# Linear attention: the squares of the outputs summed on ScalarE, the gated outputs in a buffer of their own

## The chip, the cores and the metric

The kernel runs on one core of a Trainium2 chip. The metric is the device time of one execution in microseconds (us), lower is better. Engines are named TensorE (PE), VectorE (DVE), ScalarE (ACT), GpSimd (POOL) and SyncE (SP, which here only starts transfers).

## What is computed

One layer of a hybrid decoder, for a prompt of 1024 tokens with 16 meta tokens in front and for 8 decode sequences of 4 new tokens each. A projection feeds two groups of heads: four heads of gated linear attention and eight heads of latent attention. Their outputs go through an output projection, a layer norm, a gated feed-forward with a short convolution, and another layer norm. The change touches the linear attention alone, which in the reference is:

```python
def gla_chunked(q, k, v, log_a, s0, chunk):
    ...
    def step(s, inp):
        qi, ki, vi, gi = inp
        b = jnp.cumsum(gi, axis=2)
        ...
        o_inter = jnp.einsum('bhcd,bhde->bhce', qi * jnp.exp(b), s)
        att = jnp.einsum('bhid,bhjd->bhij', qi * jnp.exp(b - b_mid), ki * jnp.exp(b_mid - b))
        att = jnp.where(causal, att, 0.0)
        o_intra = jnp.einsum('bhij,bhje->bhie', att, vi)
        s_new = s * jnp.exp(b_last)[:, :, 0, :, None] + jnp.einsum(
            'bhcd,bhce->bhde', ki * jnp.exp(b_last - b), vi)
        return s_new, o_inter + o_intra
...
def mixer_output(o_gla, g_g, o_lat, gla_norm_g, w_uv, w_o):
    gate = jax.nn.silu(g_g.reshape(B, T, GLA_HEADS, GLA_DV))
    og = (rms_norm(o_gla, gla_norm_g) * gate).reshape(B, T, GLA_HEADS * GLA_DV)
```

The root-mean-square norm of each head's output (128 values) needs the sum of its squares; the norm's factor and the gate are both multiplied onto the output.

## The kernel before

The program is written out by hand for each engine: one function per stage and engine (`pe_c`, `act_c`, `dve_c`, `pool_c` are the linear attention), called one after another. An engine runs its instructions in the order in which they are written and stops at `wait_ge(semaphore, count)` until the count is reached. So the order within an engine is fixed, and all order between engines is by semaphores. `dve_settle` and `act_settle` make an engine wait for its own last instruction before the next one.

The linear attention has nine tiles of tokens. Tile 0 has 48 rows (32 decode tokens and the 16 meta tokens), tiles 1 to 8 have 128 prompt tokens each, which are two reference chunks of 64. I call a tile a chunk below. For chunk i:

- TensorE: `scores(i)` (L707) and transposes of the decayed keys (L714); `outputs(i)` from the masked scores and the values (L738) and from the states (L751; L744 for chunk 0); `updates(i)`, the two state products (L724; L782 for chunk 0); `turn(i)`, transposes of the finished outputs (L762). From i = 2 on its order is scores(i), outputs(i-1), updates(i), turn(i-2).
- ScalarE: `kdt_copy(i)` (L811) brings the turned keys out of PSUM; `o_copy(i)` (L820) the outputs, in two instructions, into `osb[i % 2]`; `og_copy(i)` (L827) the turned outputs into `catT` with the norm's gain. Order: kdt_copy(i), o_copy(i-1), og_copy(i-2).
- VectorE: `mask(i)` (L867) copies the scores under the causal mask into `att`; `squares(i)` squares the outputs into `sq` (L891), sums each head's 128 squares into `orow` (L894) and multiplies the gate onto the outputs in place (L895); `states(i)` (L879) decays and updates the state twice; `scale(i)` (L901) multiplies the norm's factor on. Order: mask(i), squares(i-1), states(i), scale(i-1).
- GpSimd: two small instructions per chunk (L934, L935) turn the sums into the factor, from `osum_ready` to `orstd_ready`. After chunk 0 it also starts the two stores of the decode states.

`outputs(i)` waits for the masked scores of chunk i, for `o_copy(i-1)` (`osb_ready`), and for the first of the two state updates in `states(i)` (`state_ready`). The waits in it:

```python
                pe.wait_ge(att_masked, 2 * (i + 1))
                if i >= 1:
                    pe.wait_ge(osb_ready, 2 * i)
                    pe.wait_ge(state_ready, 2 + 2 * (i - 1) + 1)
```

A sum of squares on ScalarE exists elsewhere in the kernel: at L569, `ACT.Square` with `accum_out`, on rows of 384 and 256 elements, closed by a one-element copy at L571 that raises the semaphore. `accum_out` becomes an instruction of its own, ACTIVATION_READ_ACCUMULATOR. The latent attention's softmax (L1302) also uses `accum_out`. The stage after this one starts with VectorE's L1127 and TensorE's L1040, which both wait for the last `og_copy` (`og_out`).

Of the kernel before, what the change touches and what calls it, by code (L numbers as in the profile page):

```python
# [8 lines left out]
ACT = mybir.ActivationFunctionType  # L9
AX = mybir.AxisListType  # L10
# [4 lines left out]
P = 128  # L15
# [36 lines left out]
def rows(i):  # L52
    return ROWS0 if i == 0 else P
# [49 lines left out]
def build(nc, ins, outs):  # L103
    with ExitStack() as ctx:
# [541 lines left out]
        qbz = at("qbz", [P, 2, DEC_B, ROWS0], E0 + 14912)  # L646
        sq = at("sq", [P, GH, GV], E0 + 17984)
        orow = at("orow", [P, 2, 8], E0 + 20032)
# [48 lines left out]
        def pe_c(pe):  # L697
# [58 lines left out]
            def turn(i):  # L756
                r = rows(i)
                pe.wait_ge(og_ready, i + 1)
                if i >= 1:
                    pe.wait_ge(og_out, i)  # L760
                for h in range(GH):
                    last = nc.tensor.transpose(ps[:, 7, P * h:P * h + r], osb[i % 2][0:r, h // 2, h % 2, :],  # L762
                                               ident[0:r, 0:r])
                last.then_inc(og_turned, 1)
# [36 lines left out]
        def act_c(act):  # L801
# [12 lines left out]
            def o_copy(i):  # L814
                r = rows(i)
                act.wait_ge(o_done, i + 1)
                if i >= 2:
                    act.wait_ge(og_turned, i - 1)
                for h in range(2):
                    nc.scalar.activation(osb[i % 2][0:r, :, h, :],  # L820
                                         ps[0:r, 4 + h, 0:256].rearrange("p (m e) -> p m e", m=2),
                                         ACT.Copy).then_inc(osb_ready, 1)

            def og_copy(i):
# [10 lines left out]
            last.then_inc(vz_act, 1)  # L835
            o_copy(0)
            kdt_copy(1)
            for i in range(1, NT + 2):
                if 2 <= i < NT:
                    kdt_copy(i)  # L840
                if 1 <= i - 1 < NT:
                    o_copy(i - 1)
                if 0 <= i - 2 < NT:
                    og_copy(i - 2)

        def dve_c(dve):
# [37 lines left out]

            def squares(i):
                r = rows(i)
                dve.wait_ge(osb_ready, 2 * (i + 1))
                x = osb[i % 2][0:r, :, :, :].rearrange("p m h e -> p (m h) e")
                if i >= 1:
                    dve.wait_ge(osum_ready, i)  # L890
                dve_settle(nc.vector.tensor_tensor(sq[0:r, :, :], x, x, mult))  # L891
                if i >= 2:
                    dve.wait_ge(og_ready, i - 1)
                nc.vector.tensor_reduce(orow[0:r, i % 2, 0:4], sq[0:r, :, :], AX.X, add).then_inc(osum_ready, 1)  # L894
                dve_settle(nc.vector.tensor_tensor(x, x, gate_t[0:r, i, :].rearrange("p (h e) -> p h e", h=GH), mult))  # L895

            def scale(i):
                r = rows(i)
                x = osb[i % 2][0:r, :, :, :].rearrange("p m h e -> p (m h) e")
                dve.wait_ge(orstd_ready, i + 1)  # L900
                nc.vector.tensor_tensor(x, x, orow[0:r, i % 2, 4:8].unsqueeze(2).broadcast_to((r, GH, GV)),  # L901
                                        mult).then_inc(og_ready, 1)
# [6 lines left out]
            mask(1)  # L909
            squares(0)  # L910
            dve.wait_ge(o_done, 1)
# [10 lines left out]
            for i in range(2, NT + 1):  # L922
                if i < NT:
                    mask(i)
                squares(i - 1)
                if i < NT:
                    states(i)
                scale(i - 1)
# [1432 lines left out]
```

## Time and profile before

| | |
|---|---|
| median of 3 runs | 1787.85 us (1786.32 to 1788.46) |
| profiled execution, its own time | 1788.77 us |
| its span | 1787.0 us |
| mean granted TensorE clock | 0.951 of full speed |
| TensorE busy (matmul) | 1631.3 us, 91% |
| VectorE busy | 735.3 us, 41% |
| ScalarE busy | 586.9 us, 33% |
| GpSimd busy | 211.6 us, 12% |

The span is the time between the first and the last instruction in the trace; the execution's own time has some 1.8 us around it. Busy shares are means over stages that differ: the linear attention runs from about 266 to 340 us of the span, 4% of it. Times in the trace are us from the span's start. In a timeline row the number in square brackets is how long the engine had been idle before, and behind `<-` what released it; "x4" says that four like instructions are merged in the row.

### The profile page before, as it was taken

How to read it: one execution, taken by the hardware profiler on the slowest of the kernel's cores; microseconds unless marked ns; L12 is line 12 of the kernel's file. 1: busy time of each engine (PE TensorE's matmuls, PEld its weight loads, DVE VectorE, ACT ScalarE, POOL GpSimd, SP SyncE). 2: the span in 40 equal slices, each digit the busy share in tenths (PEclk: the TensorE clock that was granted, in tenths of full speed). 3: DMA queues.
4: the chain of work that ended last, by engine and by line, in shares of the span. 5: the costliest groups of instructions: out<-in, count | busy, mean ns of one | idle time of the engine just before them, and what ended most of it. 6: DMA issues, size and time to landing. Idle time of an engine off the chain costs nothing.

```text
span 1787.0 us, 26293 instructions
## 1 busy us (share of the span) xinstructions
PE 1631.3 (91%) x10609; PEld 1377.2 (77%) x10609; DVE 735.3 (41%) x1297; ACT 586.9 (33%) x1090; POOL 211.6 (12%) x313
## 2 busy tenths in 40 slices
PE   4999997898999787888979999999999979989994
PEld 4989995565666454446869999999999978768783
DVE  7325007655555333335651222222222234364744
ACT  2246212333566544442112222222222223233330
POOL 2110002103400355211110000000000000010101
PEclk9999998798999988888989999999999989999997
DMA  7202112011100555441231111111111134354530
GB/s 239 103 31 63 48 29 71 4 47 47 32 1 1 195 174 193 142 142 73 93 107 37 39 43 47 47 47 35 47 47 47 35 118 141 118 175 125 180 119 27
DMA packets 91169, 147.73 MB, mean 83 GB/s; under 512 B 6346, under 2 KB 63048, under 8 KB 91048
## 3 DMA queue, kind: packets, MB, share of 16 engines
q1 hardware_dynamic: 75242, 92.84, 16.5%
q0 software_dynamic: 15408, 52.30, 8.7%
q10 hardware_dynamic: 432, 1.37, 0.2%
q8 instruction: 62, 1.02, 0.2%
q14 instruction: 25, 0.20, 0.0%
HBM read 130.76 MB, written 15.72 MB: 82 GB/s over the span
## 4 chain that ended last, share of the span: by engine, by line
PE 67%; DVE 4%; ACT 3%; issue 1%; DMA 1%; POOL 0%; SPq 0%; ACTq 0%; DVEq 0%; POOLq 0%
PE ps L208 16%; PE ps L210 16%; PE ps L209 16%; PE ps L1241 4%; PE ps L1575 4%; PE ps L1555 3%; PE ps L1278 2%; PE ps L1601 2%; PE ps L1255 2%; ACT pastr L1652 2%; DVE d_lo L2206 1%; DVE y L306 1%; DVE y L308 1%; DVE wo_lo L1825 0%; DVE y L2185 0%
## 5 line engine op out<-in xcount | busy, mean ns | idle before, releaser
L210 PE MATMUL ps<-h1T_hi,f_lo 128*128 128x358 f32 (+1 forms) x1056 | 344.5, 326 | 0.0
L209 PE MATMUL ps<-h1T_lo,f_hi 128*128 128x358 f32 (+1 forms) x1056 | 344.3, 326 | 0.0
L208 PE MATMUL ps<-h1T_hi,f_hi 128*128 128x358 f32 (+1 forms) x1056 | 343.4, 325 | 0.0
L208 PEld LDWEIGHTS ps<-h1T_hi,f_hi 128*128 128x128 f32 x1056 | 199.3, 189 | 0.0
L210 PEld LDWEIGHTS ps<-h1T_hi,f_lo 128*128 128x128 f32 x1056 | 199.3, 189 | 0.0
L209 PEld LDWEIGHTS ps<-h1T_lo,f_hi 128*128 128x128 f32 x1056 | 199.1, 189 | 0.0
L208 PE MATMUL ps<-d_hi,g_hi 128*128 128x512 f32 x396 | 159.0, 402 | 19.2 <-DVE d_lo L2206 16.4
L209 PE MATMUL ps<-d_lo,g_hi 128*128 128x512 f32 x396 | 158.0, 399 | 0.0
L210 PE MATMUL ps<-d_hi,g_lo 128*128 128x512 f32 x396 | 157.8, 398 | 0.0
L208 PE MATMUL ps<-w_hi,hT_hi 128*128 128x256 f32 (+2 forms) x504 | 140.9, 280 | 0.0
L210 PE MATMUL ps<-w_hi,hT_lo 128*128 128x256 f32 (+2 forms) x504 | 140.3, 278 | 0.0
L209 PE MATMUL ps<-w_lo,hT_hi 128*128 128x256 f32 (+2 forms) x504 | 140.3, 278 | 0.0
L2038 DVE TENSOR_TENSOR f_lo<-f_raw,f_hi 128x1024 fp32r<-128x1024 f32 x44 | 53.7, 1221 | 201.3 <-ACT f_hi L1991 201.3
L2051 DVE SCALAR_TENSOR_TENSOR conv<-ext,vcol,conv 128x1088 f32<-128x1088 f32 x44 | 59.5, 1352 | 151.7 <-ACT conv L2023 148.7
L1991 ACT ACTIVATE f_hi<-f_raw 128x1024 fp32r<-128x1024 f32 x44 | 46.2, 1052 | 211.7 <-PE ps L210 197.6
L208 PEld LDWEIGHTS ps<-d_hi,g_hi 128*128 128x128 f32 x396 | 75.3, 190 | 40.0 <-issue 14.5
L210 PEld LDWEIGHTS ps<-w_hi,hT_lo 128*128 128x128 f32 x504 | 96.4, 191 | 0.0
L208 PEld LDWEIGHTS ps<-w_hi,hT_hi 128*128 128x128 f32 x504 | 96.2, 191 | 0.1
L209 PEld LDWEIGHTS ps<-w_lo,hT_hi 128*128 128x128 f32 x504 | 95.9, 190 | 0.0
L2204 DVE TENSOR_TENSOR g_lo<-gT,g_hi 128x384 fp32r<-128x384 f32 (+1 forms) x88 | 38.2, 455 | 139.9 <-ACT d_hi L2168 139.9
L2167 ACT ACTIVATE g_hi<-gT 128x384 fp32r<-128x384 f32 (+1 forms) x88 | 36.6, 439 | 178.5 <-PE ps L210 172.1
L210 PEld LDWEIGHTS ps<-d_hi,g_lo 128*128 128x128 f32 x396 | 75.3, 190 | 18.4
(297 smaller groups left out, 2755.5 us busy)
## 6 DMA issues: line engine op xcount, KB each, us to landing
d_raw<-in_w_down SPq DMA_DIRECT2D x66, 512.0 KB, 3.6
f_raw<-in_w_ffn_in SPq DMA_DIRECT2D x88, 256.0 KB, 3.2
w_raw<-in_w_in SPq DMA_DIRECT2D x6, 1024.0 KB, 5.2
xs<-in_x_prompt SPq DMA_DIRECT2D x8, 512.0 KB, 4.2
h_res<-xs POOLq DMA_DIRECT2D x8, 512.0 KB, 4.0
wo_raw<-in_w_o SPq DMA_DIRECT2D x2, 2048.0 KB, 8.7
hr<-h_res SPq DMA_DIRECT2D x8, 512.0 KB, 3.7
h_res<-hr POOLq DMA_DIRECT2D x8, 512.0 KB, 3.0
```

Of the source, the lines that this page charges most:

```text
L208: nc.tensor.matmul(out, ah, bh, start=start, stop=False)
L209: nc.tensor.matmul(out, ah, bl, start=False, stop=False)
L210: return nc.tensor.matmul(out, al, bh, start=False, stop=stop)
L1241: last = nc.tensor.matmul(ps[:, bank + b, 0:w], qT[0:QD, h, c:c + P], kT[0:QD, h, NS + 512 * b:NS + 512 * b + w], start=True, stop=True)
L1255: last = nc.tensor.transpose(ps[:, 4 + g % 2, P * t:P * t + P], probs[k % 2][:, P * b:P * b + P], ident)
L1555: last = nc.tensor.transpose(ps[:, n % TURN_BANKS, P * j:P * j + P], src, ident)
L1575: last = nc.tensor.matmul(ps[32 * b:32 * b + 32, bank, 0:n], q, x, start=c == 0, stop=c == 2)
L1991: nc.scalar.activation(f_hi[h][:, :, :, :], f_raw[h][:, :, :, :], ACT.Copy).then_inc(f_high, 1)
L2038: nc.vector.tensor_tensor(f_lo[h][:, :, :, :], f_raw[h][:, :, :, :], f_hi[h][:, :, :, :].bitcast(F32), sub).then_inc(f_split, 1)
L2051: last = nc.vector.scalar_tensor_tensor(out=conv[:, :], in0=ext[:, j:j + LC], scalar=vcol[:, bass.ds(c + V_ROWS["conv_w"] + j * FC, 1)], i ...
L2167: nc.scalar.activation(g_hi[m % SPL][:, o:o + n], gT[:, k, c:c + n], ACT.Copy)
L2204: nc.vector.tensor_tensor(g_lo[m % SPL][:, o:o + n], gT[:, k, c:c + n], g_hi[m % SPL][:, o:o + n].bitcast(F32), sub)
```

## The change

Three things change, all in the linear attention.

- The squares and their sums go from VectorE to ScalarE. A function `squares` in `act_c`, right behind each `o_copy`, issues four `ACT.Square` of 128 columns (one per head) with `accum_out` into `orow`, each followed by a wait on itself, and a one-element copy that raises `osum_ready`. The result of the Squares themselves goes to a scratch tile, `sq_junk`.
- The gated outputs go to a pair of buffers of their own, `ogb`, in place of `osb` in place. `scale` and TensorE's transposes work on `ogb`.
- The waits follow: `o_copy(i)` waits for `og_ready` (chunk i-2 scaled) where it waited for `og_turned` (chunk i-2 turned); the new `squares(i)` for the same; VectorE's `gated(i)`, which replaces its `squares(i)`, waits for `og_turned` (chunk i-2 turned).

```diff
--- before.py
+++ after.py
@@ -644,7 +644,8 @@
         osb = [at(f"osb{i}", [P, 2, 2, GV], E0 + 8384 + 2048 * i) for i in range(2)]
         kdt = [at(f"kdt{i}", [P, 2, P], E0 + 12864 + 1024 * i) for i in range(2)]
         qbz = at("qbz", [P, 2, DEC_B, ROWS0], E0 + 14912)
-        sq = at("sq", [P, GH, GV], E0 + 17984)
+        ogb = [at(f"ogb{i}", [P, 2, 2, GV], o) for i, o in enumerate((E0 + 17984, E0 + 47168))]
+        sq_junk = at("sq_junk", [P, GV], E0 + 49216)
         orow = at("orow", [P, 2, 8], E0 + 20032)
         sst = [at(f"sst{i}", [P, 2, GV], E0 + 21440 + 1024 * i) for i in range(4)]
 
@@ -759,7 +760,7 @@
                 if i >= 1:
                     pe.wait_ge(og_out, i)
                 for h in range(GH):
-                    last = nc.tensor.transpose(ps[:, 7, P * h:P * h + r], osb[i % 2][0:r, h // 2, h % 2, :],
+                    last = nc.tensor.transpose(ps[:, 7, P * h:P * h + r], ogb[i % 2][0:r, h // 2, h % 2, :],
                                                ident[0:r, 0:r])
                 last.then_inc(og_turned, 1)
 
@@ -815,11 +816,20 @@
                 r = rows(i)
                 act.wait_ge(o_done, i + 1)
                 if i >= 2:
-                    act.wait_ge(og_turned, i - 1)
+                    act.wait_ge(og_ready, i - 1)
                 for h in range(2):
                     nc.scalar.activation(osb[i % 2][0:r, :, h, :],
                                          ps[0:r, 4 + h, 0:256].rearrange("p (m e) -> p m e", m=2),
                                          ACT.Copy).then_inc(osb_ready, 1)
+
+            def squares(i):
+                r = rows(i)
+                if i >= 2:
+                    act.wait_ge(og_ready, i - 1)
+                for h in range(GH):
+                    last = act_settle(nc.scalar.activation(sq_junk[0:r, :], osb[i % 2][0:r, h // 2, h % 2, :], ACT.Square,
+                                                           accum_out=orow[0:r, i % 2, h:h + 1]))
+                nc.scalar.activation(sq_junk[0:r, 0:1], osb[i % 2][0:r, 0, 0, 0:1], ACT.Copy).then_inc(osum_ready, 1)
 
             def og_copy(i):
                 r, c = rows(i), col0(i)
@@ -834,12 +844,16 @@
                                             ACT.Identity, scale=consts[0:ROWS0, C_SEG + s:C_SEG + s + 1])
             last.then_inc(vz_act, 1)
             o_copy(0)
+            act.wait_ge(osb_ready, 2)
+            squares(0)
             kdt_copy(1)
             for i in range(1, NT + 2):
                 if 2 <= i < NT:
                     kdt_copy(i)
                 if 1 <= i - 1 < NT:
                     o_copy(i - 1)
+                    act.wait_ge(osb_ready, 2 * i)
+                    squares(i - 1)
                 if 0 <= i - 2 < NT:
                     og_copy(i - 2)
 
@@ -882,21 +896,18 @@
                     last.then_inc(state_ready, 1)
                     dve.wait_ge(state_ready, 2 + n + 1)
 
-            def squares(i):
+            def gated(i):
                 r = rows(i)
                 dve.wait_ge(osb_ready, 2 * (i + 1))
-                x = osb[i % 2][0:r, :, :, :].rearrange("p m h e -> p (m h) e")
-                if i >= 1:
-                    dve.wait_ge(osum_ready, i)
-                dve_settle(nc.vector.tensor_tensor(sq[0:r, :, :], x, x, mult))
                 if i >= 2:
-                    dve.wait_ge(og_ready, i - 1)
-                nc.vector.tensor_reduce(orow[0:r, i % 2, 0:4], sq[0:r, :, :], AX.X, add).then_inc(osum_ready, 1)
-                dve_settle(nc.vector.tensor_tensor(x, x, gate_t[0:r, i, :].rearrange("p (h e) -> p h e", h=GH), mult))
+                    dve.wait_ge(og_turned, i - 1)
+                dve_settle(nc.vector.tensor_tensor(ogb[i % 2][0:r, :, :, :].rearrange("p m h e -> p (m h) e"),
+                                                   osb[i % 2][0:r, :, :, :].rearrange("p m h e -> p (m h) e"),
+                                                   gate_t[0:r, i, :].rearrange("p (h e) -> p h e", h=GH), mult))
 
             def scale(i):
                 r = rows(i)
-                x = osb[i % 2][0:r, :, :, :].rearrange("p m h e -> p (m h) e")
+                x = ogb[i % 2][0:r, :, :, :].rearrange("p m h e -> p (m h) e")
                 dve.wait_ge(orstd_ready, i + 1)
                 nc.vector.tensor_tensor(x, x, orow[0:r, i % 2, 4:8].unsqueeze(2).broadcast_to((r, GH, GV)),
                                         mult).then_inc(og_ready, 1)
@@ -907,7 +918,7 @@
                                                consts[0:ROWS0, C_SEG + s:C_SEG + s + 1], None, mult)
             last.then_inc(vz_ready, 1)
             mask(1)
-            squares(0)
+            gated(0)
             dve.wait_ge(o_done, 1)
             for m in range(2):
                 dve.wait_ge(u_done, m + 1)
@@ -922,7 +933,7 @@
             for i in range(2, NT + 1):
                 if i < NT:
                     mask(i)
-                squares(i - 1)
+                gated(i - 1)
                 if i < NT:
                     states(i)
                 scale(i - 1)
```

**VectorE, one prompt chunk in the steady part, before.** `sq` and `osb` are the squares and the outputs, `sst` the states, `att` the masked scores:

```order
L891 TENSOR_TENSOR sq<-osb_108 128x512 [waits osum_ready,osb_ready]
L894 TENSOR_REDUCE orow<-sq 128x4 [waits og_ready,dve_step]
L895 TENSOR_TENSOR osb_108<-osb_108,gate_t 128x512
L879 SCALAR_TENSOR_TENSOR sst_116<-sst_115,ebl,ps 128x128 [waits o_done,u_done,dve_step]
L879 SCALAR_TENSOR_TENSOR sst_116<-sst_115,ebl,ps 128x128
L879 SCALAR_TENSOR_TENSOR sst_117<-sst_116,ebl,ps 128x128 [waits o_done,u_done,state_ready]
L879 SCALAR_TENSOR_TENSOR sst_117<-sst_116,ebl,ps 128x128
L901 TENSOR_TENSOR osb_108<-osb_108,orow 128x512 [waits orstd_ready,state_ready]
L867 COPY_PREDICATED att_106<-gmask,ps 128x128 [waits o_done,att_done]
```

**VectorE, the same place now.** `ogb` is the new buffer of gated outputs:

```order
L904 TENSOR_TENSOR ogb_113<-osb_108,gate_t 128x512 [waits og_turned,osb_ready]
L893 SCALAR_TENSOR_TENSOR sst_118<-sst_117,ebl,ps 128x128 [waits o_done,u_done,dve_step]
L893 SCALAR_TENSOR_TENSOR sst_118<-sst_117,ebl,ps 128x128
L893 SCALAR_TENSOR_TENSOR sst_119<-sst_118,ebl,ps 128x128 [waits o_done,u_done,state_ready]
L893 SCALAR_TENSOR_TENSOR sst_119<-sst_118,ebl,ps 128x128
L912 TENSOR_TENSOR ogb_113<-ogb_113,orow 128x512 [waits orstd_ready,state_ready]
L881 COPY_PREDICATED att_106<-gmask,ps 128x128 [waits o_done,att_done]
```

Two instructions and the waits between them are gone in front of the state updates; the scale and the mask behind it stand where they stood, and the scale still waits for `orstd_ready`.

**ScalarE, the same kind of chunk, before:**

```order
L811 ACTIVATE kdt_110<-ps 128x256 [waits u_done,kd_turned]
L820 ACTIVATE osb_109<-ps 128x2x128 [waits og_turned,o_done]
L820 ACTIVATE osb_109<-ps 128x2x128
L827 ACTIVATE catT<-ps,vcol 128x4x128 [waits og_turned]
```

**ScalarE now:**

```order
L812 ACTIVATE kdt_110<-ps 128x256 [waits u_done,kd_turned]
L821 ACTIVATE osb_109<-ps 128x2x128 [waits og_ready,o_done]
L821 ACTIVATE osb_109<-ps 128x2x128
L830 ACTIVATE sq_junk,orow<-osb_109 128x128 [waits og_ready,osb_ready]
L830 ACTIVATE sq_junk,orow<-osb_109 128x128 [waits act_step] x3
L832 ACTIVATE sq_junk<-osb_109 128x1 [waits act_step]
L837 ACTIVATE catT<-ps,vcol 128x4x128 [waits og_turned]
```

Between the copy of the outputs and the copy of turned outputs there are five more instructions (and an accumulator read after each of the four Squares, which this view doesn't list).

## Rows read from the trace of the kernel before

**Rows 1.** The page, part 4: shares of the span by engine.
```profile
PE 67%; DVE 4%; ACT 3%; issue 1%; DMA 1%; POOL 0%; SPq 0%; ACTq 0%; DVEq 0%; POOLq 0%
```

**Rows 2.** Stretch, its us; busy PE, PEld, DVE, ACT, POOL; PEclk, DMA, GB/s.
```profile
291.50:334.20 42.70, 32.95 (x359) 24.25 (x352) 31.99 (x80) 11.45 (x28) 11.00 (x14) 0.86 0.09 29
```

**Rows 3.** Timeline of one prompt chunk: start us, duration us, engine, line, operation.
```profile
303.06 0.66 ACT L820 ACTIVATE osb<-ps 128x256 f32<-128x256 f32 x2 [2.55 <-PE ps L751]
...
303.75 0.69 DVE L891 TENSOR_TENSOR sq<-osb 128x512 f32<-128x512 f32 x1 [0.82 <-ACT osb L820]
...
304.65 0.44 PE L714 MATMUL ps<-consts,t_b 128*128 128x128 f32 x2
...
305.08 0.68 DVE L895 TENSOR_TENSOR osb<-osb,gate_t 128x512 f32<-128x512 f32 x1
...
305.80 1.25 DVE L879 SCALAR_TENSOR_TENSOR sst<-sst,ebl,ps 128x128 f32<-128x128 f32 x4
...
306.55 0.68 PE L738 MATMUL ps<-v_t,att 128*128 128x128 f32 x4 [1.46 <-DVE sst L879]
...
307.08 0.69 DVE L901 TENSOR_TENSOR osb<-osb,orow 128x512 f32<-128x512 f32 x1
...
307.69 0.89 DVE L867 COPY_PREDICATED att<-gmask,ps 128x128 f32<-128x128 int32 x4
...
308.70 0.66 ACT L820 ACTIVATE osb<-ps 128x256 f32<-128x256 f32 x2 [3.19 <-PE ps L751]
```

**Rows 4.** Timeline of ScalarE: the other six output copies of prompt chunks.
```profile
290.94 0.66 ACT L820 ACTIVATE osb<-ps 128x256 f32<-128x256 f32 x2 [2.92 <-PE ps L751]
...
297.42 0.66 ACT L820 ACTIVATE osb<-ps 128x256 f32<-128x256 f32 x2 [4.15 <-PE ps L751]
...
315.72 0.66 ACT L820 ACTIVATE osb<-ps 128x256 f32<-128x256 f32 x2 [4.58 <-PE ps L751]
...
321.36 0.66 ACT L820 ACTIVATE osb<-ps 128x256 f32<-128x256 f32 x2 [3.10 <-PE ps L751]
...
327.65 0.66 ACT L820 ACTIVATE osb<-ps 128x256 f32<-128x256 f32 x2 [3.84 <-PE ps L751]
...
333.52 0.66 ACT L820 ACTIVATE osb<-ps 128x256 f32<-128x256 f32 x2 [3.25 <-PE ps L751]
```

**Rows 5.** Timeline of ScalarE at 106 to 121 us: Squares with an accumulator.
```profile
108.05 0.53 ACT L569 ACTIVATE junk<-zt 128x384 f32<-128x384 f32 x1
...
108.69 0.42 ACT L569 ACTIVATE junk<-zt 128x256 f32<-128x256 f32 x1
...
109.24 0.52 ACT L569 ACTIVATE junk<-zt 128x384 f32<-128x384 f32 x1
...
118.76 0.20 ACT L571 ACTIVATE junk<-zt 128x1 f32<-128x1 f32 x1
```

**Rows 6.** Groups of ScalarE by line and shape: busy us, mean ns | idle.
```profile
L1302 ACT ACTIVATION_READ_ACCUMULATOR probs<-ps,mx 128x1 f32 x66 | 13.3, 201 | 0.0
...
L1302 ACT ACTIVATE probs<-ps,mx 128x128 f32<-128x128 f32 x8 | 2.9, 365 | 0.0
```

**Rows 7.** Timeline where the stage starts (chunk 0).
```profile
276.48 0.65 ACT L820 ACTIVATE osb<-ps 48x256 f32<-48x256 f32 x2 [5.33 <-PE ps L744]
...
277.37 4.09 PE L782 MATMUL ps<-vz,kdt 48*64 48x512 f32 x24
...
279.94 2.15 DVE L915 SCALAR_TENSOR_TENSOR s_in<-s_in,ebl,ps 128x128 f32<-128x128 f32 x8
```

**Rows 8.** Timeline where the stage ends.
```profile
334.94 0.69 DVE L894 TENSOR_REDUCE orow<-sq 128x4 f32<-128x512 f32 x1
...
335.71 0.56 POOL L934 TENSOR_SCALAR orow<-orow 128x4 f32<-128x4 f32 x1 [4.22 <-DVE orow L894]
...
337.46 0.69 DVE L901 TENSOR_TENSOR osb<-osb,orow 128x512 f32<-128x512 f32 x1 [1.25 <-POOL orow L935]
...
340.08 0.49 DVE L1127 TENSOR_SCALAR w_uqn<-w_uq_sb,vcol 128x512 f32<-128x512 f32 x1 [1.93 <-ACT catT L827]
```

## The prediction

> **What bounds the kernel now.** I read four views in this order. The chain that ended last comes first: 67% of the span is TensorE [rows 1]. The change touches only the linear attention stage, so I ask whether TensorE sets the pace there too. The busy time by stretch says no: over the eight prompt chunks TensorE has work in 33.0 of 42.7 us, VectorE in 32.0, ScalarE in 11.5 [rows 2]. No engine is full, so the chunk runs at the pace of a loop of waits. The timeline of one chunk shows the loop [rows 3]: ScalarE copies the outputs (303.06, 0.66 us); VectorE squares them (303.75), sums, gates (305.08), then updates the states (305.80); TensorE, which waited for the first state, starts the next outputs (306.55); the next copy starts at 308.70. Period: 5.64 us.
>
> The stretches of this loop, from the same rows: copy start to square 0.69; square to gate 1.33 (square and row sum); gate to state update 0.72; state update to TensorE 0.75; TensorE to the next copy 2.15. Gate start to next copy start is thus 3.62.
>
> Not every chunk has this pace. The eight copies start at 290.94, 297.42, 303.06, 308.70, 315.72, 321.36, 327.65 and 333.52 [rows 3, 4]: periods of 6.48, 5.64, 5.64, 7.02, 5.64, 6.29, 5.87. Less 0.69 + 1.33 = 2.02, the parts from gate start to next copy are 4.46, 3.62, 3.62, 5.00, 3.62, 4.27 and 3.85. The longer ones are TensorE's at a lower clock: 0.86 granted in this stretch [rows 2], so about a quarter of it ran at 1.2 GHz and the rest at 2.4.
>
> **The change, part by part.**
>
> *Removed from VectorE:* square and row sum, 1.33 us of the loop per chunk. If nothing took their place, the loop would be 5.64 - 1.33 = 4.31 us at the full clock; seven periods give 9.3 us.
>
> *Added to ScalarE:* four Square instructions of 128 elements, each followed by its accumulator read and a wait on itself, and a one-element copy that signals. The same construction runs earlier in the kernel with 384 and 256 elements [rows 5]: start to start 0.64 (108.05 to 108.69) and 0.55 (108.69 to 109.24), read and wait included. 128 elements fewer cost 0.10, so at 128 I take 0.445 each, 1.78 for four. The one-element copy takes 0.20. Upper bound: the shortest activation with an accumulator, 128 elements out of PSUM, takes 0.365, and its read 0.201 [rows 6]: 0.566. Lower bound: 0.33, one of the two 256-element halves of the output copy without accumulator. The three differ mostly in overlap; I take 0.445 because it is the same instruction, operand memory and wait.
>
> *Where that lies:* ScalarE has room: busy 11.45 us in the eight chunks, 1.4 each [rows 2], and 1.98 more makes 3.4 of 4.31; and the next output copy waits for TensorE. But the row sums now come later. From a copy's start: 0.66 copy, 0.03 hand-over (as 303.72 to 303.75), 1.78 squares, 0.20 signal, 0.08 to GpSimd: 2.75. GpSimd's two instructions and the hand-over take 1.75 (335.71 to 337.46) [rows 8], so VectorE can scale that chunk 4.50 us after the copy began. It is ready for it much sooner (the state updates end some 0.69 + 0.72 + 1.25 = 2.7 us after it), so **a new wait appears**: VectorE stands at the scale for up to 1.9 us, where before GpSimd's answer was in before it came there. Behind the scale in VectorE's order stand the mask of the chunk after next and then the next chunk's gate. Scale to mask is 0.61, the mask 0.89 (307.08, 307.69) [rows 3]. So the next chunk's gate can't start before 4.50 + 1.50 = 6.00 us after the previous chunk's copy began. With gate to copy 3.62 this is a loop over two chunks of 6.00 + 3.62 = 9.62, or 4.81 each. It is longer than 4.31 and sets the average pace.
>
> *The walk, with the measured TensorE parts.* Gate = the later of (own copy + 0.69) and (previous copy + 6.00); next copy = gate + its part. From a first copy at 290.50 (next paragraph) the copies come at 295.65, 300.12, 305.27, 311.12, 315.42, 321.39 and 325.93. Before, the last was at 333.52, so this is 7.59 earlier, 0.44 of it from the start of the stage.
>
> *Start of the stage.* Chunk 0 loses 1.33 us in front of VectorE's first big update at 279.94, but that also waits for TensorE's first six pairs of state products: 24 matmuls of 4.09 us from 277.37, so half are done at 279.4 [rows 7]. Gain: 0.44, not 1.33. ScalarE's copy of chunk 1's keys now stands behind four squares: 277.13 + 0.03 + 1.98 + 0.33 = 279.5. TensorE wants it at 279.4; lost 0.1, off VectorE's path. The first prompt chunk's copy starts at 290.94 - 0.44 = 290.50.
>
> *End of the stage.* After the last copy (333.52) the row sum ends at 334.94 + 0.69, and the scale starts at 337.46, 3.94 after the copy [rows 4, 8]. Now 4.50: lost 0.56. After that ScalarE's last copy and the next stage follow directly: VectorE's first instruction there (340.08) waited for that copy [rows 8], so the shift is handed on whole.
>
> *The buffer of its own and the swapped waits* cost nothing: the transpose reads the new buffer at the same place in each order, and the copy's new condition (the chunk two back is scaled) is met before the gate of the chunk in between. No transfer is added.
>
> **Sum:** -0.44 (start) - 7.15 (seven periods) + 0.56 (end) = -7.0 us. The profiled execution took 1788.77 in all (span 1787.0), giving 1781.8; it lay 0.9 above the median of the runs shown, 1787.85, from which I forecast **1780.8**.
>
> **A rule weighed against the rows.** In rows 5 the Squares take 0.53 and 0.42 us; the slope leaves about 0.32 for 128 elements without the accumulator read. The Trainium skill (VectorE: DVE Perf Modes, the section on the TRN2 errata) gives a ScalarE instruction from SBUF 224 cycles plus one per element, an estimate of 0.29 us here, and warns that many small tiles pay the fixed part each time. By 0.29 a Square, with its read wholly hidden, the walk would give 9.0 us gained and 1778.8 in place of 1780.8; by the rows the read isn't hidden, so the rows' sum stays.
>
> **The rivals.**
>
> 1. *The wait at the scale hardly binds, or TensorE speeds up.* Without the 6.00 bound the same walk gives 9.2 us (1778.7). With the bound but TensorE at 2.4 GHz all the way (3.62 each) it gives 9.3. Both together would give 12.3 (1775.6). For it: TensorE's idle gaps shrink. Against: 4.50 is built from measured pieces. Chance 0.15.
>
> 2. *TensorE becomes the bound, or a Square costs the upper price.* At the full clock TensorE finishes the last transposes of a chunk's scores at 305.09 (304.65 + 0.44), 2.03 after the copy's start, while the shortened loop wants its next outputs at 0.69 + 1.47 = 2.16: only 0.13 to spare, none at 1.2 GHz. With 0.566 per Square the gain is 4.9 us; with all seven parts at 5.00, 2.6. That is 1783.0 to 1785.3. Chance 0.12.
>
> 3. *Slower than before: VectorE is held at the scale longer than it saved.* Place: the scale in VectorE's order, behind ScalarE's squares and GpSimd. Each extra 0.1 us per Square lengthens the two-chunk loop by 0.4 and the end by 0.4; it also holds up ScalarE's copy of chunk 1's keys at the start. The walk turns from gain to loss at about 0.82 us per Square, and at 1.0 gives +3.8, 1791.6. It would take Squares delayed by VectorE's gate reading the same tile at that moment. Against: no activation with accumulator of this size takes over 0.57 with its read. The Trainium skill (ScalarE: Activation LUTs, the rules for kernel authors) says to keep multiplications off ScalarE; that points this way, and no row of this case bears it out at this size. Chance 0.03.
>
> 4. *The gain is given back.* The next stages start 7 us earlier, and TensorE's lower clock falls on other work, or a transfer isn't there yet. Time 1787 to 1788. Against: the first instructions of the next stage wait for ScalarE, not for a transfer [rows 8]. Chance 0.05.
>
> The forecast itself has 0.65.
>
> **How the numbers follow.** Differences under 0.2% (3.6 us) can't be told from none: the border is 1784.3. Faster: 0.65 + 0.15 + half of the second rival (0.06) = 0.86. Within: the other 0.06 + 0.05 = 0.11. Slower: 0.03. The range reaches down to 1777.0, past most of the first rival, and up to 1784.5, into the second, which leaves out somewhat under 2 in 10.
>
> **What would show it.** Per chunk: four Squares with reads in about 1.8 us; VectorE idle before the scale, ended by GpSimd, some 1 to 1.9 us in most chunks; gate starts alternating between 4.3 and 5.4 us apart; first copy to last 35.4 us in place of 42.6; the last copy to the last scale 4.5. The forecast is wrong if the average period is under 4.6 or over 5.6, or if the stage is 7 us shorter and the span isn't.

## The result, and the profile after

The changed kernel took 1776.22 us (median of 6 runs, 1771.75 to 1779.43) beside 1787.41 (6 runs, 1782.21 to 1788.46) for the kernel before: ratio 0.994, 95% interval 0.9921 to 0.9958. Two later groups of runs gave 0.9933 (0.9908 to 0.9957) and 0.9933 (0.9912 to 0.9955). It is faster, as forecast, but by 11 us and not by 7: the median lies 0.8 us under the range (1777.0 to 1784.5). The profiled execution took 1779.43.

The page as a whole hardly moved. Its part 1 and the first line of part 4:

```profile
PE 1628.7 (92%) x10609; PEld 1375.9 (77%) x10609; DVE 723.0 (41%) x1279; ACT 601.4 (34%) x1171; POOL 208.1 (12%) x313
...
PE 67%; DVE 4%; ACT 3%; issue 1%; DMA 1%; POOL 0%; SPq 0%; ACTq 0%; DVEq 0%; POOLq 0%
```

ScalarE has 14.5 us more work and 81 instructions more, VectorE 12.3 us less, and the chain is TensorE's for the same 67% [rows 1]. The stage says more. Its busy time over the eight prompt chunks (same columns as [rows 2]: length, PE, PEld, DVE, ACT, POOL, then PEclk, DMA share, GB/s):

```profile
292.60:324.40 31.80, 27.95 (x355) 20.17 (x350) 22.40 (x66) 22.77 (x91) 8.43 (x14) 1.00 0.12 39
```

The stretch is 31.8 us long where it was 42.7, and the granted clock is 1.00 where it was 0.86. TensorE has work in 28.0 of 31.8 us. One pair of periods in the timeline of the changed kernel, to be laid beside [rows 3]:

```profile
301.17 0.66 ACT L821 ACTIVATE osb<-ps 128x256 f32<-128x256 f32 x2 [1.36 <-PE ps L752]
...
301.86 0.69 DVE L904 TENSOR_TENSOR ogb<-osb,gate_t 128x512 f32<-128x512 f32 x1
...
301.86 0.31 ACT L830 ACTIVATE sq_junk<-osb 128x128 f32<-128x128 f32 x1
...
302.07 0.19 ACT L830 ACTIVATION_READ_ACCUMULATOR sq_junk<-osb 128x1 f32 x1
...
302.29 0.31 ACT L830 ACTIVATE sq_junk<-osb 128x128 f32<-128x128 f32 x1
...
303.34 0.68 PE L739 MATMUL ps<-v_t,att 128*128 128x128 f32 x4
...
303.59 0.20 ACT L832 ACTIVATE sq_junk<-osb 128x1 f32<-128x1 f32 x1
...
303.88 0.19 POOL L945 TENSOR_SCALAR orow<-orow 128x4 f32<-128x4 f32 x1 [3.54 <-ACT sq_junk L832]
...
304.15 1.01 POOL L946 TENSOR_TENSOR orow<-orow,mhalf 128x4 f32<-128x4 f32 x1
...
305.27 0.69 DVE L912 TENSOR_TENSOR ogb<-ogb,orow 128x512 f32<-128x512 f32 x1 [1.44 <-POOL orow L946]
...
305.49 0.66 ACT L821 ACTIVATE osb<-ps 128x256 f32<-128x256 f32 x2 [0.84 <-PE ps L752]
...
305.87 0.89 DVE L881 COPY_PREDICATED att<-gmask,ps 128x128 f32<-128x128 int32 x4
...
306.67 0.68 DVE L904 TENSOR_TENSOR ogb<-osb,gate_t 128x512 f32<-128x512 f32 x1
...
307.39 1.25 DVE L893 SCALAR_TENSOR_TENSOR sst<-sst,ebl,ps 128x128 f32<-128x128 f32 x4
...
308.14 0.68 PE L739 MATMUL ps<-v_t,att 128*128 128x128 f32 x4 [0.24 <-DVE sst L893]
...
308.20 0.19 POOL L945 TENSOR_SCALAR orow<-orow 128x4 f32<-128x4 f32 x1 [3.04 <-ACT sq_junk L832]
...
310.29 0.66 ACT L821 ACTIVATE osb<-ps 128x256 f32<-128x256 f32 x2 [1.32 <-PE ps L752]
```

Two periods of three engines stand here, row by row in order of time. The gate (L904) starts 0.69 us after the copy (L821), with no square and row sum in front of it. The Squares come every 0.43 us. VectorE then stands at the scale for 1.44 us until GpSimd is done (305.27), does the mask (305.87), and only then, at 306.67, the next gate, though its copy began at 305.49. The periods are 4.32 (301.17 to 305.49) and 4.80 (305.49 to 310.29). All seven: 4.32, 4.84, 4.32, 4.80, 4.32, 4.80, 4.32, in all 31.72 us; before 42.58 [rows 3, 4]. The mean period is 4.53 us, under the 4.6 that the prediction named as a sign of being wrong.

The end of the stage, in the same view:

```profile
323.73 0.66 ACT L821 ACTIVATE osb<-ps 128x256 f32<-128x256 f32 x2 [1.12 <-PE ps L752]
...
327.83 0.69 DVE L912 TENSOR_TENSOR ogb<-ogb,orow 128x512 f32<-128x512 f32 x1 [2.72 <-POOL orow L946]
...
330.45 0.49 DVE L1138 TENSOR_SCALAR w_uqn<-w_uq_sb,vcol 128x512 f32<-128x512 f32 x1 [1.93 <-ACT catT L837]
```

From the last copy to the last scale it takes 4.10 us (3.94 before), and the next stage starts 2.62 us later, as before (337.46 to 340.08) [rows 8].

### The profile page after: what moved, and what is told of

Same layout as the page of the kernel before. It is cut to its first block, busy times and chain, and to the rows that moved or that the text cites. A ratio compares the mean times of both kernels' runs of the same rounds, so it can differ in the third digit from the quotient of the medians.

```text
span 1777.6 us, 26355 instructions
## 1 busy us (share of the span) xinstructions
PE 1628.7 (92%) x10609; PEld 1375.9 (77%) x10609; DVE 723.0 (41%) x1279; ACT 601.4 (34%) x1171; POOL 208.1 (12%) x313
## 4 chain that ended last, share of the span: by engine, by line
PE 67%; DVE 4%; ACT 3%; issue 1%; DMA 1%; POOL 0%; SPq 0%; ACTq 0%; DVEq 0%; POOLq 0%
PE ps L208 16%; PE ps L210 16%; PE ps L209 16%; PE ps L1252 4%; PE ps L1586 4%; PE ps L1566 4%; PE ps L1289 2%; PE ps L1612 2%; PE ps L1266 2%; ACT pastr L1663 2%; DVE d_lo L2217 1%; DVE y L306 1%; DVE y L308 1%; DVE wo_lo L1836 0%; DVE y L2196 0%
## 5 line engine op out<-in xcount | busy, mean ns | idle before, releaser
L208 PEld LDWEIGHTS ps<-d_hi,g_hi 128*128 128x128 f32 x396 | 75.5, 191 | 39.8 <-issue 14.5
```

Of the source, the lines that this page charges most:

```text
L208: nc.tensor.matmul(out, ah, bh, start=start, stop=False)
```

## The experiments

Three groups of runs followed the result, each beside the kernel before on its own chip: before and changed again, slowed and mask first; then buffers alone, gate in place, Squares twice and square beside GpSimd; then changed a third time, mask first again, order alone and states first. "Copies" is the time from the start of the first to the start of the last output copy of the eight prompt chunks, seven periods, in the profiled execution of each; "clock" is TensorE's granted clock from the end of the first copy to the start of the last; "out" is the start of the next stage's first VectorE instruction.

| kernel | median us | ratio to before (95%) | copies us | clock | out us |
|---|---|---|---|---|---|
| before | 1787.41 | | 42.58 | 0.87 | 340.08 |
| before again | 1786.43 | 0.9991 (0.9971 to 1.0012) | 44.80 | 0.80 | 341.54 |
| changed | 1776.22 | 0.9940 (0.9921 to 0.9958) | 31.72 | 1.00 | 330.45 |
| changed again | 1774.55 | 0.9933 (0.9908 to 0.9957) | 31.73 | 1.00 | 327.56 |
| changed, third | 1773.46 | 0.9933 (0.9912 to 0.9955) | 31.73 | 1.00 | 328.73 |
| slowed | 1787.15 | 1.0008 (0.9986 to 1.0029) | 44.11 | 0.85 | 343.19 |
| buffers alone | 1885.21 | 0.9992 (0.9969 to 1.0015) | 40.51 | 0.96 | 336.31 |
| gate in place | 1893.26 | 1.0036 (1.0017 to 1.0055) | 49.28 | 0.82 | 346.83 |
| Squares twice | 1888.20 | 1.0007 (0.9984 to 1.0029) | 39.26 | 0.94 | 341.67 |
| square beside GpSimd | 1875.07 | 0.9942 (0.9922 to 0.9961) | 33.33 | 1.00 | 331.93 |
| mask first | 1773.28 | 0.9928 (0.9903 to 0.9952) | 30.24 | 1.00 | 327.74 |
| mask first again | 1774.83 | 0.9940 (0.9919 to 0.9960) | 30.25 | 1.00 | 329.13 |
| order alone | 1779.12 | 0.9971 (0.9956 to 0.9987) | 34.61 | 0.95 | 334.96 |
| states first | 1768.38 | 0.9906 (0.9884 to 0.9928) | 28.42 | 1.00 | 327.29 |

The kernel before had medians of 1786.91, 1885.84 and 1784.63 in the three groups. The chip of the second group ran every kernel 5 to 6% longer. Later stages held the stalls that were seen (with the buffers alone ScalarE's L1306 sat idle for 18.9 us at once), and their cause was not looked for. Of this group the ratios and the copies are used, not the times.

**1. Before and changed, once more.** No edit. The question is whether the low clock in the chunks belongs to the kernel before.

> The kernel before, unchanged, timed against itself and profiled once more. Question: were the long TensorE parts of its chunks (first to last output copy 42.58 us, 39.5 if all were at 2.4 GHz) its own, or the chance of one execution? Theory A (TensorE idles enough in each 5.6 us period that its clock drops again and again): the mean granted clock between the first and the last copy of the prompt chunks is again clearly under 1.00, and copy to copy 41 to 44 us. Theory B (chance of the moment): it may be 1.00, and 39.5 us. Time 1787 us, ratio 1.000 within 0.002.

> The changed kernel, unchanged, timed and profiled once more. Theory A: granted clock 1.00 between the first and last output copy again, seven periods alternating between 4.32 and 4.82 us, 31.7 us in all. Theory B: some low stretches, 32 to 35 us. GpSimd's first instruction 0.19 us again. Time 1776 us, ratio to before 0.994.

> The changed kernel a third time: ratio to before 0.9935 within 0.002; the granted clock in the chunks 1.00, periods alternating between 4.32 and 4.8 us, 31.7 us for the seven.

Busy time between the first and the last copy, before again:

```profile
290.84:334.98 44.14, 34.56 (x349) 25.41 (x348) 31.98 (x80) 10.69 (x26) 11.01 (x14) 0.80 0.08 28
```

The changed kernel again:

```profile
289.77:320.84 31.07, 27.31 (x348) 19.71 (x344) 21.93 (x66) 22.06 (x88) 8.45 (x14) 1.00 0.12 40
```

The clock is 0.80 in one and 1.00 in the other, as in the first pair, and 1.00 in the third profile of the changed kernel. The long periods of the kernel before fell elsewhere (7.17, 5.64, 6.49, 5.64, 5.64, 7.04, 7.18), but they are there again. Its shortest period is 5.64 both times. Theory A, that the low clock belongs to this loop and not to the chance of one execution, stands.

**2. Slowed.** The removed work is put back in front of the gate, into tiles that nobody reads:

```diff
             def gated(i):
...
+                x = osb[i % 2][0:r, :, :, :].rearrange("p m h e -> p (m h) e")
+                dve_settle(nc.vector.tensor_tensor(sqd[0:r, :, :], x, x, mult))
+                dve_settle(nc.vector.tensor_reduce(sumd[0:r, 0:GH], sqd[0:r, :, :], AX.X, add))
                 dve_settle(nc.vector.tensor_tensor(ogb[i % 2][0:r, :, :, :].rearrange("p m h e -> p (m h) e"),
```

> The changed kernel with VectorE's square and row sum put back in front of the gate, into tiles nobody reads (the computation is unchanged otherwise). The loop is 5.64 us again, TensorE idles as before. Theory A (the clock follows from TensorE's idle share): the granted clock between first and last copy falls under 1.00 again, 41 to 44 us, and the whole kernel is back at 1786 to 1788 us. Theory B (chance): clock 1.00, 39.5 us, about 1784 us.

```profile
293.01:336.46 43.45, 32.80 (x349) 23.95 (x350) 32.64 (x80) 22.17 (x88) 8.44 (x14) 0.85 0.09 28
```

Theory A came: clock 0.85, copies 44.11 us, and the whole kernel back at 1787.15. Only the shortest period is not 5.64 as expected but 5.76. The whole gain hangs on the length of this loop. Seven periods of 5.76 would be 40.3 us; nearly all of the other 3.8 lie in three periods of 6.77 to 7.25, in which the granted clock was 0.75 to 0.82.

**3. Mask first.** VectorE's next mask moves into the idle time before the scale:

```diff
+            mask(2)
             for i in range(2, NT + 1):
-                if i < NT:
-                    mask(i)
                 gated(i - 1)
                 if i < NT:
                     states(i)
+                if i + 1 < NT:
+                    mask(i + 1)
                 scale(i - 1)
```

> The changed kernel with VectorE's mask of the next-but-one chunk moved in front of the scale. My theory: the longer of the two alternating periods (4.8 us) comes from the chain signal, GpSimd, scale, mask, gate; with the mask in the idle time before the scale the chain is 0.9 us shorter and no longer binds, so all seven periods are 4.32 us, 30.2 us in place of 31.7, and the kernel is about 1.5 us faster than the changed one. Rival: the mask now runs beside GpSimd's instructions and makes them longer (0.56 in place of 0.19 for the first), or TensorE is the bound by then; then 31 us or more and no gain.

> The kernel with the mask moved, once more beside the changed kernel on one chip: 4.32 us in all seven periods, 30.2 us; ratio to before 0.992 to 0.993, and 0.0005 to 0.001 under the changed kernel's, less than this measurement can tell.

```profile
291.43:321.01 29.58, 27.54 (x348) 19.94 (x348) 23.07 (x66) 22.06 (x89) 8.44 (x14) 1.00 0.13 42
```

Seven periods of 4.32, 30.24 and 30.25 us, in both runs: the short loop of the prediction (4.31). So the longer of the alternating periods was the chain through GpSimd, the scale and the mask. The rival, that the mask beside GpSimd makes its instruction longer, didn't come: the mask starts at 302.11, GpSimd's instruction at 302.13, and it takes 0.19 us. The 1.5 us can't be told in the whole kernel's time; they are shown by the copies alone.

**4. The buffers alone.** Squares and sums stay on VectorE; the transposes and the scale use `ogb` here too (not shown):

```diff
+        ogb = [at(f"ogb{i}", [P, 2, 2, GV], E0 + 47168 + 2048 * i) for i in range(2)]
...
-                    act.wait_ge(og_turned, i - 1)
+                    act.wait_ge(og_ready, i - 1)
...
-                dve_settle(nc.vector.tensor_tensor(x, x, gate_t[0:r, i, :].rearrange("p (h e) -> p h e", h=GH), mult))
+                if i >= 2:
+                    dve.wait_ge(og_turned, i - 1)
+                y = ogb[i % 2][0:r, :, :, :].rearrange("p m h e -> p (m h) e")
+                dve_settle(nc.vector.tensor_tensor(y, x, gate_t[0:r, i, :].rearrange("p (h e) -> p h e", h=GH), mult))
```

> The kernel before with the gated outputs in buffers of their own and the waits that go with them; the squares and sums stay on VectorE. My theory: the buffers give nothing alone, since VectorE still works through square, sum and gate in front of the state updates: shortest period 5.64 us, GpSimd's first instruction 0.56 us, time as before, ratio 1.000 within 0.002. Rival: the waits for the buffers held something up (or let something through), and the periods change.

Ratio 0.9992, periods of 5.64 but for one of 6.67. The buffers give nothing alone. Its clock of 0.96 shows how far the loop of the kernel before can be lucky: 40.51 us.

**5. The gate in place.** Squares on ScalarE, no buffer of its own; the transposes, the scale and the wait of the output copy are as in the kernel before (not shown):

```diff
-                if i >= 2:
-                    dve.wait_ge(og_turned, i - 1)
-                dve_settle(nc.vector.tensor_tensor(ogb[i % 2][0:r, :, :, :].rearrange("p m h e -> p (m h) e"),
+                dve.wait_ge(osum_ready, i + 1)
+                dve_settle(nc.vector.tensor_tensor(osb[i % 2][0:r, :, :, :].rearrange("p m h e -> p (m h) e"),
```

> The changed kernel without the buffer of its own: ScalarE sums the squares, the gate is multiplied in place and so has to wait for the sums. My theory: gate start moves from 0.69 to about 2.65 us after the copy's start (0.66 copy, 1.76 squares, 0.20 signal, hand-over), and the shortest period is 2.65 + 3.63 = 6.3 us, 44 us or more for the seven, longer than the 5.64 of the kernel before; 1788 to 1794 us in all, slower than before by 0.1 to 0.4%. Rival: the squares moved off VectorE are what counts and the buffer is a detail; then the time stays near 1776.

One copy, the signal of the sums and the gate in its timeline:

```profile
304.82 0.66 ACT L821 ACTIVATE osb<-ps 128x256 f32<-128x256 f32 x2 [2.52 <-PE ps L752]
...
307.25 0.20 ACT L832 ACTIVATE sq_junk<-osb 128x1 f32<-128x1 f32 x1
...
307.55 0.72 DVE L903 TENSOR_TENSOR osb<-osb,gate_t 128x512 f32<-128x512 f32 x1 [2.85 <-ACT sq_junk L832]
```

The gate starts 2.73 us after the copy, the shortest period is 6.38, and three of the seven are 7.92. The kernel is slower than before by 0.17 to 0.55%. VectorE is busy for only 23.2 of the 49.3 us here, and the clock is 0.82: it went with the long loop, not with VectorE's amount of work. The two parts of the change need each other: the buffer is worth nothing alone, the move is worth less than nothing without it.

**6. Every Square twice.**

```diff
-                for h in range(GH):
+                for h in range(2 * GH):
+                    h %= GH
```

> The changed kernel with every Square done twice (eight per chunk, the second set writes the same sums again). My theory of the two loops: 1.74 us more between copy and scale lengthens only the loop over two chunks, from 9.14 to 10.9 us, so the periods alternate between about 4.3 and 6.5 us, 37.0 us for the seven at the full clock in place of 31.7, the last copy to the last scale 5.85 in place of 4.1, the start about 1.5 later: 8.5 us more than the changed kernel, 1784 to 1788 us (the upper end if the clock falls). Rival, the squares lie beside other work: no change. Rival, everything is in one loop: 7 x 1.74 = 12.2 us more in the periods.

ScalarE's timeline over one pair of periods:

```profile
304.85 0.66 ACT L821 ACTIVATE osb<-ps 128x256 f32<-128x256 f32 x2 [0.85 <-PE ps L752]
...
305.54 0.31 ACT L831 ACTIVATE sq_junk<-osb 128x128 f32<-128x128 f32 x1
...
309.01 0.20 ACT L833 ACTIVATE sq_junk<-osb 128x1 f32<-128x1 f32 x1
...
309.12 0.67 ACT L838 ACTIVATE catT<-ps,vcol 128x512 f32<-128x512 f32 x1
...
309.69 0.38 ACT L812 ACTIVATE kdt<-ps 128x256 f32<-128x256 f32 x1
...
309.95 0.66 ACT L821 ACTIVATE osb<-ps 128x256 f32<-128x256 f32 x2
...
315.71 0.66 ACT L821 ACTIVATE osb<-ps 128x256 f32<-128x256 f32 x2 [0.54 <-PE ps L752]
```

Two periods take 5.10 + 5.76 = 10.86 us, as the loop over two chunks says (10.9), and from the last copy to the last scale it takes 5.84. The alternation is flatter than I expected, since ScalarE has become the bound of the short period: the copy at 309.95 has no idle time in front of it. The copies take 39.26 us, not 37.0: the first six periods are 32.63 as expected, the seventh is 6.63, at a granted clock of 0.71. The start of the stage was missed too. From chunk 0's copy to the first prompt copy it takes 17.40 us, beside 14.1 to 14.7 in the three profiles of the changed kernel, so about 3 us more and not 1.5: ScalarE's copy of chunk 1's keys stands behind eight Squares until 280.80, and TensorE waits 1.71 us for it. The ratio, 1.0007, is 0.7% over the changed kernel's, 12 to 13 us; I had expected 8.5 to 12. The parts agree with it: 7.5 (periods) + 1.7 (end) + about 3 (start). A Square is free only as long as VectorE gets the scale's factor in time.

**7. A square beside GpSimd.** In both profiles of the kernel before GpSimd's first instruction took 0.56 us and in the changed one 0.19 us, on the same four numbers per row. The groups of GpSimd, before and after:

```profile
L934 POOL TENSOR_SCALAR orow<-orow 128x4 f32<-128x4 f32 x8 | 4.5, 561 | 37.4 <-DVE orow L894 37.4
```

```profile
L945 POOL TENSOR_SCALAR orow<-orow 128x4 f32<-128x4 f32 x8 | 1.6, 194 | 29.7 <-ACT sq_junk L832 29.7
```

Theory C of the next expectation puts that down to VectorE's gate beside it. To find out, VectorE gets one more square, with two operands in SBUF and a result that nobody reads, in its idle time:

```diff
                 if i < NT:
                     states(i)
+                x = osb[(i - 1) % 2][:, :, :, :].rearrange("p m h e -> p (m h) e")
+                dve_settle(nc.vector.tensor_tensor(sqd[:, :, :], x, x, mult))
                 scale(i - 1)
```

> The changed kernel with one more VectorE square with two operands in SBUF (result unused) placed in its idle time between the state updates and the scale, where GpSimd works on the sums. Theory C (GpSimd's first instruction took 0.56 us before because VectorE's gate with two SBUF operands ran beside it): in the chunks where the two overlap it takes 0.4 to 0.8 us in place of 0.19, and the scale behind it starts that much later. Theory D (it was 0.56 for another reason): 0.19 in all eight chunks, periods as in the changed kernel, 31.7 us for the seven. Time within 2 us of the changed kernel either way.

Two chunks in its timeline:

```profile
304.26 0.69 DVE L942 TENSOR_TENSOR sqd<-osb 128x512 f32<-128x512 f32 x1
...
304.28 0.73 POOL L949 TENSOR_SCALAR orow<-orow 128x4 f32<-128x4 f32 x1 [4.08 <-ACT sq_junk L834]
...
305.09 1.01 POOL L950 TENSOR_TENSOR orow<-orow,mhalf 128x4 f32<-128x4 f32 x1
...
306.20 0.69 DVE L914 TENSOR_TENSOR ogb<-ogb,orow 128x512 f32<-128x512 f32 x1 [1.24 <-POOL orow L950]
...
308.60 0.19 POOL L949 TENSOR_SCALAR orow<-orow 128x4 f32<-128x4 f32 x1 [2.50 <-ACT sq_junk L834]
...
309.60 0.69 DVE L942 TENSOR_TENSOR sqd<-osb 128x512 f32<-128x512 f32 x1
```

Where the square (304.26 to 304.95) runs beside it, GpSimd's instruction takes 0.73 us and ends with it; where the square comes a microsecond later (309.60), 0.19. Four of the eight chunks are of the first kind, and the long periods grow from 4.80 to 5.34. Theory C is shown: the square alone was added, and GpSimd's instruction is long in just the chunks where it overlaps. The Trainium skill (GPSIMD Engine Reference, section 1, Specifications) says that GpSimd shares its SBUF interfaces with VectorE and contends with VectorE instructions that have two SBUF inputs; the trace agrees, with 0.73 against 0.19. The state updates, with one of their two tensors in PSUM, don't do it: in the changed kernel's timeline above they run from 307.39 to 308.64 and GpSimd's instruction at 308.20 takes 0.19.

**8. Order alone, states first.** One edit, made to the kernel before (there with `squares` in place of `gated`) and to the changed one:

```diff
+            mask(2)
             for i in range(2, NT + 1):
-                if i < NT:
-                    mask(i)
-                gated(i - 1)
                 if i < NT:
                     states(i)
+                gated(i - 1)
+                if i + 1 < NT:
+                    mask(i + 1)
                 scale(i - 1)
```

> The kernel before (squares, sums and gate all on VectorE, in place) with VectorE's order alone changed: the state updates of chunk i in front of square, sum and gate of chunk i-1, and the next mask in front of the scale. My theory: what made the loop long was not how much VectorE does but what stood between the output copy and the state updates. With this order the state updates wait only for TensorE, and the period falls to VectorE's own work, 0.89 + 1.25 + 2.05 + 0.69 and the gaps, about 5.1 to 5.3 us in place of 5.64: 36 to 37 us for the seven, some 5 to 8 us less than before (42.6 and 44.8), ratio 0.995 to 0.997. Rival: the loop's length comes from VectorE's amount of work beside TensorE, and order changes nothing; 40.5 us or more.

```profile
292.90:326.85 33.95, 27.52 (x350) 20.93 (x348) 31.00 (x79) 10.69 (x27) 9.57 (x13) 0.95 0.11 36
```

The kernel before with its order alone changed takes 34.61 us for the copies, 8 to 10 less than before, and is faster by 0.29% (0.13 to 0.44). It has every square still on VectorE. That is more than I expected. The periods run from 3.60 to 7.42, three of them are 5.07 to 5.27 at a clock of 1.00, and the one of 7.42 ran at 0.77, the lowest; so a part of this gain too came with the clock. From the last copy to the last scale (332.34) it takes 5.49 us, 1.55 more than before.

> The changed kernel with the same new order on VectorE: state updates, gate, next mask, scale. In the changed kernel with the mask moved alone TensorE was busy 27.5 of 29.6 us, so little is left: my theory is that TensorE is the bound and the periods fall from 4.32 only to 4.1 to 4.25, 29.3 us for the seven; the whole kernel within 1.5 us of the one with the mask moved, no difference that can be measured. Rival: some other wait (ScalarE's squares in front of its next copies) holds it at 4.32 or longer.

```profile
292.80:320.56 27.76, 26.10 (x352) 19.86 (x348) 22.58 (x65) 22.04 (x88) 7.76 (x14) 1.00 0.13 45
```

28.42 us, under the 29.3 that I gave TensorE: TensorE is busy 26.1 of 27.8 us, so it is close to the bound, but the periods (3.76, 4.64, 3.94, 4.42, 3.94, 4.42, 3.30) alternate, not constant at 4.2 as expected. At 0.9906 it is the fastest of all. Against the changed kernel's 0.9933 in the same group the intervals overlap, so only the copies (3.3 us less) show it surely. The expectation for the whole kernel failed: it was to lie within 1.5 us of mask first and lies 6.5 us under it (1768.38 and 1774.83, 5 and 6 runs). The copies explain 1.8 us of that; the rest is open.

## Why the prediction was wrong by 4 us

**The loop and its shortening: right.** 5.64 became 4.31 in the forecast and 4.32 in the trace; gate start to next copy, 3.62 forecast, 3.63 measured (301.86 to 305.49). The slowed kernel and mask first show both ends of it.

**The new wait at the scale and the loop over two chunks: right in kind.** VectorE waits 1.44 us there, periods alternate, gates are 4.3 and 4.8 us apart.

**The term that was mis-sized is the seven periods: -7.15 in the sum, -10.86 measured.** It failed in two places. The step that failed is pricing the new loop from rows of the old one: TensorE's parts at the old loop's lower clock, and GpSimd's instruction beside the old gate. Two stretches of the kernel before, around its period of 7.02 us (308.70 to 315.72), show the clock, the third figure from the end (0.57 is a mean: from 312.5 to 315.5 us it was 0.50):

```profile
308.00:312.00 4.00, 2.73 (x41) 1.91 (x39) 3.12 (x8) 1.73 (x4) 1.02 (x2) 1.00 0.01 4
312.00:316.00 4.00, 3.81 (x40) 3.06 (x40) 2.14 (x8) 0.28 (x1) 0.55 (x1) 0.57 0.00 0
```

Over that whole period it was 0.76, over the periods of 5.64 on either side 1.00.

- *TensorE's parts.* The walk took the seven parts as measured, 3.62 to 5.00, although I had just read that the long ones were TensorE at a lower clock. The long parts were not a property of the work but went with the loop: in the seven profiles whose mean period was 4.1 to 4.8 us the clock was 1.00 (changed three times, mask first twice, states first, the square beside GpSimd), in the five whose periods were all 5.6 us or more it was 0.80 to 0.96. Between them lie the order alone (mean 4.94, 0.95) and the Squares twice (mean 5.61, 0.94). With 3.62 for all seven the same walk gives 4.31 + 3 x 9.62 = 33.2 us, 2.3 less than 35.4. I had this as the first rival and gave it 0.15; its 9.3 us were closer than the forecast's 7.0. The same rival without the bound gives 12.3 us, nearer still to the measured 11.2, but the bound does bind, so that nearness would have been luck.
- *The bound of 6.00 us from a copy to the next gate.* Measured: 2.42 + 0.29 + 1.39 + 1.40 = 5.50 (copy to signal, signal to GpSimd, GpSimd to scale, scale to gate). Forecast: 2.47 + 0.28 + 1.75 + 1.50. Of the 0.50 missed, 0.37 is GpSimd's first instruction, which I took at 0.56 us from a row in which VectorE's gate ran beside it. Most of the rest is 0.10 between scale and gate: 1.40 is less than the 1.50 that I added from starts and a duration, since the gate starts (306.67) before the mask has ended (305.87 + 0.89). With 5.50 the walk gives 4.31 + 3 x 9.12 = 31.7 us, and 31.72 is measured.

**Squares: right.** 0.445 forecast, 0.43 measured. The lower price by the Trainium skill's figure (VectorE: DVE Perf Modes, the errata section: an estimate of 0.29 us for a 128-element ScalarE instruction) fits the Square itself, 0.31 us; what it leaves out is the read behind it and the wait.

**Start and end.** The end lost 0.16 us, not 0.56, again GpSimd's instruction. The start gained less than the 0.44 forecast as far as it can be read. From chunk 0's output copy to VectorE's first big update it takes 3.46 and 3.47 us in the two profiles before and 3.21 in all three after, 0.25 less, and the update now waits for TensorE, as forecast. Up to the first prompt copy the rest is lost in spread: 14.46 and 14.48 us before, 14.22, 14.09 and 14.67 after.

**Handed on whole: right as far as it can be read.** The next stage starts at 340.08 and 341.54 before, at 330.45, 327.56 and 328.73 after: 340.8 against 328.9 in the mean, 11.9 us. The medians differ by 11.2, 12.4 and 11.2. Nothing is given back. From that point to the end of the span the two profiles before took 1446.9 and 1447.1 us, the three after 1447.2, 1442.5 and 1442.9; whether those 4 us in two of them are gained elsewhere or chance isn't shown.

**The rival on the other side** didn't come, but its mechanism is real: with the Squares twice, 0.87 us per head, the gain is gone (1.0007), where I had put the point of no gain at about 0.82 us. Of the kernels run, only the gate in place is slower than before.

**What stays open:** how much of the gain is the clock alone. Seven periods of 5.64, the shortest, would be 39.5 us. The kernel before took 42.58 and 44.80, and with the buffers alone, the same loop, 40.51: 1 to 5 us more, 3 in the mean. So I estimate the clock's part at some 3 of the 11 us. No run held the clock fixed, and a lower clock doesn't always cost: in the second profile of the kernel before one period of 5.64 ran at 0.72.

## What to carry to other kernels

Find the loop of waits first, and ask what stands in it between one result and the next release: taking VectorE's work out of that place paid (the changed kernel), and so did moving it behind the release (the order alone), for the same reason. When a loop becomes shorter, don't carry stretches over that were measured at a lower TensorE clock or beside another engine's work: price them from their fastest rows and keep the slow ones for the range. And when a step is moved to another engine, check that the tile it reads is not then overwritten by the step that used to follow it.

## What the runs showed of the hardware

- GpSimd's four-element-wide instruction takes 0.19 us with no such neighbour and 0.56 to 0.73 when it starts inside a VectorE instruction with two SBUF operands; it then ends with it. With the gate in place it starts 0.02 us ahead of the gate (307.53 and 307.55) and takes 0.20; it is the second one, its `pow`, that starts inside the gate, and it takes 1.32 us in place of 1.01. Its group there:

```profile
L945 POOL TENSOR_TENSOR orow<-orow,mhalf 128x4 f32<-128x4 f32 x8 | 10.6, 1322 | 0.7
```

- TensorE's granted clock fell to 1.2 GHz now and then in the kernel before (0.50 of full speed from 312.5 to 315.5 us), where TensorE had work in about 33 of 42.7 us [rows 2] and stood 1.46 us before its outputs in a period of 5.64 [rows 3]. The Trainium skill (TensorE: Matmul & The Clock Gate, Why this matters for your kernels) warns of longer idle gaps between bursts; here shorter ones, as the 1.46 us of this period, went with it. With work in 28.0 of 31.8 us it was 1.00.
- A Square of 128 elements with its accumulator read and a wait on itself comes every 0.43 us, of which 0.31 is the Square.
